# Weight chunks of the feed-forward, merge and output products: five matmuls (3 x 320, 512, 256 columns) in place of six of 288, with VectorE adding the two parts of the last 256 tokens

## The reference, cut to what matters

```python
def swiglu(x, w_in, w_out):
    gate, up = jnp.split(x @ w_in, 2, axis=-1)
    return (jax.nn.silu(gate) * up) @ w_out

def hybrid_layer(x, p, attn_fn, ...):
    x = x + 0.5 * swiglu(rms_norm(x, p['ffn1_norm']), p['ffn1_w_in'], p['ffn1_w_out'])
    h = rms_norm(x, p['mix_norm'])
    ... # attention (o_a), gated recurrence (o_b), short convolution (o_c)
    gates = jax.nn.sigmoid(g.reshape(n, t, N_BRANCH, D_MODEL))
    merged = (gates[:, :, 0] * (o_a @ wb[:WIDTH_A])
              + gates[:, :, 1] * (o_b @ wb[WIDTH_A:WIDTH_A + WIDTH_B])
              + gates[:, :, 2] * (o_c @ wb[WIDTH_A + WIDTH_B:]))
    x = x + merged @ p['w_out']
    x = x + 0.5 * swiglu(rms_norm(x, p['ffn2_norm']), p['ffn2_w_in'], p['ffn2_w_out'])
```

## Time and profile before

| what | value |
|---|---|
| median of 3 runs | 3013.25 us (3011.82 to 3015.27) |
| the profiled execution | 3012.57 us |
| its span, first to last instruction | 3010.9 us |
| TensorE, matmuls | 2959.2 us busy (98%), 21632 records |
| VectorE | 1465.2 us (49%) |
| ScalarE | 985.3 us (33%) |
| GpSimd | 119.0 us (4%) |
| HBM | 82 GB/s over the span |
| granted TensorE clock, mean | 0.991 of full |

### The profile page before, as it was taken

The page is one execution under the profiler, slowest core; times in us unless marked ns, Lnnn a source line. Parts: engine busy times, 40 slices in busy tenths (PEclk is TensorE's granted clock), DMA queues, the critical chain, the costliest instruction groups (busy, mean ns, idle before and its releaser), DMA issues.

```text
span 3010.9 us, 54957 instructions
## 1 busy us (share of the span) xinstructions
PE 2959.2 (98%) x21632; PEld 2862.5 (95%) x21632; DVE 1465.2 (49%) x2025; ACT 985.3 (33%) x1287; POOL 119.0 (4%) x104
## 2 busy tenths in 40 slices
PE   7999998999999999999999999989999999999999
PEld 6999998888899999999999999988888999999998
DVE  4434355555744544343444444566665454444434
ACT  4212133444633342121332111334445333321113
POOL 1000011000000010000100000100000000000001
PEclk9999999999999999999999999999999999999999
DMA  3222222333222222222222222223332222222222
GB/s 116 84 85 79 77 82 81 84 82 82 71 82 79 91 84 83 75 80 84 85 84 73 88 86 78 84 69 83 81 82 80 84 84 91 73 86 80 84 84 87
DMA packets 299022, 248.82 MB, mean 83 GB/s; under 512 B 20643, under 2 KB 296307, under 8 KB 298919
## 3 DMA queue, kind: packets, MB, share of 16 engines
q1 hardware_dynamic: 296775, 242.44, 26.0%
q0 software_dynamic: 2144, 4.98, 0.5%
HBM read 240.04 MB, written 7.34 MB: 82 GB/s over the span
## 4 chain that ended last, share of the span: by engine, by line
PE 94%; DVE 2%; ACT 1%; issue 1%; DVEq 0%; DMA 0%; POOLq 0%; ACTq 0%; SPq 0%
PE ps L448 85%; PE ps L671 2%; PE ps L616 2%; PE ps L700 1%; DVE tmp L1019 1%; PE ps L661 1%; PE ps L647 1%; PE ps L594 1%; PE ps L617 1%; PE ps L603 0%; PE ps L552 0%; PE ps L553 0%; PE ps L554 0%; DMA xin<-in_x_sample 0%; ACT whi L759 0%
## 5 line engine op out<-in xcount | busy, mean ns | idle before, releaser
L759 ACT ACTIVATE whi<-wraw 128x1024 fp32r<-128x1024 f32 (+1 forms) x456 | 475.1, 1044 | 1610.1 <-PE ps L448 1560.9
L448 PE MATMUL ps<-hh,whi 128*128 128x288 f32 x4480 | 967.1, 298 | 18.5 <-ACT vtok L857 6.1
L448 PE MATMUL ps<-hh,wlo 128*128 128x288 f32 x4480 | 961.9, 296 | 0.0
L448 PE MATMUL ps<-hl,whi 128*128 128x288 f32 x4480 | 961.5, 296 | 0.0
L1013 DVE TENSOR_TENSOR wlo<-wraw,whi 128x1024 fp32r<-128x1024 f32 (+1 forms) x456 | 548.4, 1205 | 457.4 <-ACT whi L759 456.3
L448 PEld LDWEIGHTS ps<-hh,whi 128*128 128x128 f32 x4480 | 724.9, 190 | 25.1 <-ACT vtok L857 6.3
L448 PEld LDWEIGHTS ps<-hh,wlo 128*128 128x128 f32 x4480 | 724.5, 189 | 0.0
L448 PEld LDWEIGHTS ps<-hl,whi 128*128 128x128 f32 x4480 | 724.3, 189 | 0.0
L1047 DVE TENSOR_TENSOR tmp<-tmp,ps 128x576 f32<-128x576 f32 x176 | 132.7, 754 | 509.3 <-PE ps L448 508.4
L448 PE MATMUL ps<-al,whi 128*128 128x288 f32 x1408 | 302.2, 296 | 0.0
L448 PE MATMUL ps<-ah,whi 128*128 128x288 f32 x1408 | 302.1, 296 | 0.0
(11 more groups left out here) (282 smaller groups left out, 2519.8 us busy)
## 6 DMA issues: line engine op xcount, KB each, us to landing
wraw<-in_ffn_w_in SPq DMA_DIRECT2D x88, 1024.0 KB
wraw<-in_ffn_w_out SPq DMA_DIRECT2D x32, 1024.0 KB
wraw<-in_w_in SPq DMA_DIRECT2D x28, 1024.0 KB
wraw<-in_w_in SPq DMA_DIRECT2D x56, 512.0 KB
wraw<-in_ffn_w_out SPq DMA_DIRECT2D x16, 768.0 KB
wraw<-in_w_branch SPq DMA_DIRECT2D x24, 512.0 KB
wraw<-in_w_out SPq DMA_DIRECT2D x9, 1024.0 KB
kv<-in_cache_k SPq DMA_DIRECT2D x128, 64.0 KB, 1.9
```

Source lines behind the costliest of these rows:

```text
L448: last = pe.matmul(ps[slot][:, half, 0:HF], weights, rhs[:, k, half * HF:(half + 1) * HF], start=(start and c == 0 and n == 0), stop=(stop ...
L759: act.activation(split_tile(whi, j, rowwise), raw_tile(slot, j, rowwise), ACT.Copy).then_inc(hi_ready, 1)
```

## The change

A chunk's 1728 columns are dealt out anew. The first 320 tokens (`NA`) go through three matmuls into the second part of bank 0 (columns 192 to 511). The last 256 (`NB`) go through one matmul of 512 columns, the high weight over the high part and the remainder side by side, which lands in bank 1 as two sums of 256, and one of 256 columns, the low weight over the high part, which is added to the first of the two. For that the high part and the remainder lie in one buffer (`hb`, `ab`, `ob`, `mb`). VectorE then has to add the second sum of 256: `scaled` multiplies 576 contiguous columns (192 to 767 of the slot) by the norm or the gate, multiplies the 256 of the second sum, and adds the two, with a drain before each step; `update` has a second multiply-add of 256 columns. The slot is freed by the last of these. The values and pairs stages go on with halves of 288.

```diff
@@ -37,6 +37,8 @@
+NA = 320
+NB = N - NA
...
-        hh = sb("hh", [P, KD, N], F32R)
-        hl = sb("hl", [P, KD, N], F32R)
+        hb = sb("hb", [P, 2, KD, N], F32R)
+        hh, hl = hb[:, 0, :, :], hb[:, 1, :, :]
...
+        def flat(k):
+
+            return ps[k][:, :, :].rearrange("p b n -> p (b n)")[:, 512 - NA:512 + NB]
+
...
-            def project(slot, w, chunks, rhs_hi, rhs_lo, start=True, stop=True, before=None):
-
+            def project(slot, w, chunks, buf, hi=0, before=None):
+
+                wide, both, rest = ps[slot][:, 0, 512 - NA:512], ps[slot][:, 1, 0:2 * NB], ps[slot][:, 1, 0:NB]
                 for c, k in enumerate(chunks):
                     if before is not None:
                         before(c)
                     wh, wl = whi[:, w % 2, c * P:(c + 1) * P], wlo[:, w % 2, c * P:(c + 1) * P]
-                    for n, (weights, rhs) in enumerate(((wh, rhs_hi), (wh, rhs_lo), (wl, rhs_hi))):
+                    first, end = c == 0, c == len(chunks) - 1
+                    pe.matmul(wide, wh, buf[:, hi, k, 0:NA], start=first, stop=False)
+                    pe.matmul(wide, wh, buf[:, 1 - hi, k, 0:NA], start=False, stop=False)
+                    pe.matmul(wide, wl, buf[:, hi, k, 0:NA], start=False, stop=end)
+                    pe.matmul(both.rearrange("p (a n) -> p a n", a=2), wh, buf[:, :, k, NA:N], start=first, stop=end, skip_group_check=True)
+                    last = pe.matmul(rest, wl, buf[:, hi, k, NA:N], start=False, stop=end, skip_group_check=True)
+                return last
...
+            def scaled(out, slot, by, spare):
+
+                dve.tensor_tensor(out, by, flat(slot), ALU.mult)
+                dve.drain()
+                dve.tensor_tensor(spare[:, 0:NB], by[:, NA:N], ps[slot][:, 1, NB:2 * NB], ALU.mult)
+                dve.drain()
+                return dve.tensor_tensor(out[:, NA:N], out[:, NA:N], spare[:, 0:NB], ALU.add)
...
-                        dve.scalar_tensor_tensor(out=two(xm), in0=cols(st.slot(k)), scalar=half, in1=two(xm), op0=ALU.mult, op1=ALU.add)\
+                        dve.scalar_tensor_tensor(out=xm, in0=flat(st.slot(k)), scalar=half, in1=xm, op0=ALU.mult, op1=ALU.add)
+                        dve.drain()
+                        dve.scalar_tensor_tensor(out=xm[:, NA:N], in0=ps[st.slot(k)][:, 1, NB:2 * NB], scalar=half, in1=xm[:, NA:N],
+                                                 op0=ALU.mult, op1=ALU.add)\
                             .then_inc(freed[st.slot(k)], 1)
...
-                            dve.tensor_tensor(two(pf[:, 0:N]), two(tmp[6][:, 0:N]), cols(st_in.slot(k)), ALU.mult)\
-                                .then_inc(freed[st_in.slot(k)], 1)
+                            scaled(pf[:, 0:N], st_in.slot(k), tmp[6][:, 0:N], tmp[2]).then_inc(freed[st_in.slot(k)], 1)
...
-                                dve.tensor_tensor(two(tmp[j][:, 0:N]), cols(mg.slot(k)), two(tmp[6][:, 0:N]), ALU.mult)\
+                                scaled(tmp[j][:, 0:N], mg.slot(k), tmp[6][:, 0:N], tmp[3])\
                                     .then_inc(freed[mg.slot(k)], 1)
...
-                                t = two(tmp[2 + j][:, 0:N])
-                                dve.tensor_tensor(t, two(tmp[j - 2][:, 0:N]), cols(mg.slot(k)), ALU.mult).then_inc(freed[mg.slot(k)], 1)
+                                t = tmp[2 + j][:, 0:N]
+                                scaled(t, mg.slot(k), tmp[j - 2][:, 0:N], tmp[3]).then_inc(freed[mg.slot(k)], 1)
```

More of the change, by code:

```diff
@@ L184, in build @@
         with ExitStack() as m:
[L185 to L186 removed]
+            ab = sb("ab", [P, 2, 8, N], F32R, m)
+            ah, al = ab[:, 0, :, :], ab[:, 1, :, :]
         with ExitStack() as m:
@@ L445, in project, with halves @@
                     wh, wl = whi[:, w % 2, c * P:(c + 1) * P], wlo[:, w % 2, c * P:(c + 1) * P]
-                    for n, (weights, rhs) in enumerate(((wh, rhs_hi), (wh, rhs_lo), (wl, rhs_hi))):
+                    first, end = c == 0, c == len(chunks) - 1
[5 more added lines that the diff above has]
+                return last
+            def halves(slot, w, chunks, start=True, stop=True):
+                for c, k in enumerate(chunks):
+                    wh, wl = whi[:, w % 2, c * P:(c + 1) * P], wlo[:, w % 2, c * P:(c + 1) * P]
+                    for n, (weights, rhs) in enumerate(((wh, hh), (wh, hl), (wl, hh))):
                         for half in range(2):
@@ L450, in project, with plain, plain_halves @@
                 return last
-            def plain(st, k, w, chunks, rhs_hi, rhs_lo, L, i=0, before=None):
+            def plain(st, k, w, chunks, buf, hi, L, i=0, before=None):
                 wait_weights(st, w, L, i)
                 wait_psum(st, k, L, i)
-                project(st.slot(k), w, chunks, rhs_hi, rhs_lo, before=before).then_inc(filled[st.slot(k)], 1)
+                project(st.slot(k), w, chunks, buf, hi, before=before).then_inc(filled[st.slot(k)], 1)
+            def plain_halves(st, k, w, L, i=0):
+                wait_weights(st, w, L, i)
+                wait_psum(st, k, L, i)
+                halves(st.slot(k), w, range(KD)).then_inc(filled[st.slot(k)], 1)
             def norm(st, n, L):
@@ L493, in ffn @@
                         for k in range(4):
-                            plain(st_out, k, k, range(kc), ah, al, L, i, before=hidden_ready if k == 0 else None)
+                            plain(st_out, k, k, range(kc), ab, 0, L, i, before=hidden_ready if k == 0 else None)
             pe.wait_ge(x_loaded, X_LOADS * 16)
@@ L595, in _ @@
                         last.then_inc(filled[pr.slot(k)], 1)
-                    plain(pr, 5, 3, range(KD), hh, hl, L, p)
-                    plain(pr, 6, 4, range(KD), hh, hl, L, p)
+                    plain_halves(pr, 5, 3, L, p)
+                    plain_halves(pr, 6, 4, L, p)
                     pe.wait_ge(kv_loaded, it * 512 + 256)
@@ L639, in _ @@
                     last.then_inc(filled[pr.slot(13)], 1)
-                    plain(pr, 14, 5, range(KD), hh, hl, L, p)
+                    plain_halves(pr, 14, 5, L, p)
                     pe.wait_ge(xc_ready, it + 1)
@@ L684, in _ @@
                     wait_psum(pr, 20, L, p)
-                    project(pr.slot(20), 6, range(4), hh, hl, stop=False)
+                    halves(pr.slot(20), 6, range(4), stop=False)
                     wait_weights(pr, 7, L, p)
-                    project(pr.slot(20), 7, range(4, KD), hh, hl, start=False).then_inc(filled[pr.slot(20)], 1)
+                    halves(pr.slot(20), 7, range(4, KD), start=False).then_inc(filled[pr.slot(20)], 1)
                     pe.wait_ge(vp_ready, it + 1)
@@ L716, in _ @@
                         for j in range(2):
-                            plain(mg, 4 * b + j, 4 * b + j, range(KD), hh, hl, L, i)
+                            plain(mg, 4 * b + j, 4 * b + j, range(KD), hb, 0, L, i)
                         pe.wait_ge(o_ready, L * 12 + 4 * (b + 1))
                         for j in range(2, 4):
-                            plain(mg, 4 * b + j, 4 * b + j, range(4 * b, 4 * b + 4), oh, ol, L, i)
+                            plain(mg, 4 * b + j, 4 * b + j, range(4 * b, 4 * b + 4), ob, 1, L, i)
                 with pe.Fori(0, 2) as i:
                     for k in range(4):
-                        plain(S["out"], k, k, range(KD), mh, ml, L, i, before=(lambda c: pe.wait_ge(m_ready, L * 8 + (c + 1))) if k == 0 else None)
+                        plain(S["out"], k, k, range(KD), mb, 1, L, i, before=(lambda c: pe.wait_ge(m_ready, L * 8 + (c + 1))) if k == 0 else None)
                 ffn("ffn2", 2, L)
@@ L1387, in _ @@
                             dve.wait_ge(gate_ready, L * 24 + i * 6 + (2 * b + j - 1))
-                            mt = merged[:, bass.ds(i * 2 + (j - 2), 1), :].rearrange("p a (b n) -> p (a b) n", b=2)
+                            mt = chunk(merged, i * 2 + (j - 2))
                             if b == 0:
-                                dve.tensor_tensor(mt, two(tmp[j - 2][:, 0:N]), cols(mg.slot(k)), ALU.mult).then_inc(freed[mg.slot(k)], 1)
+                                scaled(mt, mg.slot(k), tmp[j - 2][:, 0:N], tmp[3]).then_inc(freed[mg.slot(k)], 1)
                                 dve.drain()
                             else:
-                                t = two(tmp[2 + j][:, 0:N])
-                                dve.tensor_tensor(t, two(tmp[j - 2][:, 0:N]), cols(mg.slot(k)), ALU.mult).then_inc(freed[mg.slot(k)], 1)
+                                t = tmp[2 + j][:, 0:N]
+                                scaled(t, mg.slot(k), tmp[j - 2][:, 0:N], tmp[3]).then_inc(freed[mg.slot(k)], 1)
                                 dve.drain()
```

23 lines of the change are left out of this document (12 added, 11 removed).

## The result

The changed kernel takes 3030.65 us, the median of 4 runs (3027.34 to 3033.26); the kernel before takes 3012.98 us beside it, the median of 4. The ratio is 1.0057, with a 95% interval from 1.0042 to 1.0072: 17.7 us slower, where 3013.4 was forecast, and outside the range of 3003 to 3028. The profiled execution took 3030.31 us (span 3028.6), against 3012.57 (span 3010.9).

What follows compares the result with a forecast made beforehand. TensorE, busy for 98% of the span, was taken as the bound: matmul count times pace. Gain of 33.6 us kept and 33.7 us added give +0.1 us on the profiled 3012.57, median forecast 3013.4 us, range 3003 to 3028.

Steps and rivals of the forecast that it cites:

- One instruction's 13.3 ns is saved: Feed-forward, merge and output matmuls: a chunk falls from 800 to 786.7 ns, 2816 chunks worth 37.5 us.
- The term of what is added: VectorE's added operations make TensorE wait in feed-forwards, merge, output and layer turn: 33.7 us in all.
- e: VectorE's extra time for a `scaled`, two more operations of 256 columns with their gaps: 0.98 us.
- The merge groups: Merge: VectorE's addition delays the next group's weight split, 18.5 us over 22 groups, plus 1.3 in each layer's first group.
- The wait for the last of the merged values: Merge to output: three `scaled` lengthen TensorE's wait for `ml` from 1.0 to near 3 us, 5.9 us added.
- The in-tiles of steady state: Feed-forward in-tiles: VectorE's added work is covered with 0.5 us left, so TensorE doesn't wait.
- The turn of the layers: Turn of the layers and end: second multiply-add half covered by ScalarE's copy, 2 x 0.25 = 0.5 us, an estimate.
- the term for the starts of the feed-forwards: Four feed-forward starts, where TensorE already waits for the third tile's split: 4 x 0.98 = 3.9 us added.
- The gain lost beside waits: In 294 of 2816 chunks, just ahead of TensorE's waits, shorter matmuls give nothing; 33.6 of 37.5 us are kept.
- Rival 1: Slower: VectorE's two small operations cost more than their columns, e = 1.34, 13.7 us added, 3027; chance 0.15.
- Rival 2: Slower: only 2.5 ns go with a matmul instruction, not 13.3; 27.3 us lost, 3041; chance 0.08.
- Rivals 3 and 4: Faster: chains grow less, e = 0.76, 3005, chance 0.17; long streams hide the 13.3 ns, about 2904, chance 0.05.

Runs made afterwards that it cites:

- Experiment 1: Changed kernel with only the first VectorE operation kept in `scaled` and `update`, so the second sums are left out: 2989.95 us, ratio 0.9919 to the kernel before.
- experiment 5: Five one-run variants of the changed kernel's matmuls: 512 split into two 256s 3013.84 us, 512 read in one piece 3029.73, three other orders 3038.33, 3031.72, 3031.89.
- Experiment 2: Kernel before, six matmuls kept, with VectorE's added 256-column operations behind each multiply, results unused: 3050.09 us, ratio 1.0118.
- experiment 4: Changed kernel with ScalarE's weight copy moved ahead of the second gate's sigmoid in the merge: 3007.62 us; control, the same exchange in the kernel before: 3012.54 us.

## Why the prediction was wrong

- **The step that failed is "One instruction's 13.3 ns is saved"**, the term of -37.5 us (33.6 kept). Experiment 1 measures it at 23.2 us, so 14.3 us of it weren't there (4.5 either way). The working took the overhead of 288 and 256 columns and carried it to 512, which no row showed; 320 with 256 bears the rule out (experiment 5), the chunk with 512 doesn't. The traces account for nearly all of it: 2816 x 3.3 ns = 9.4 us since a chunk saves 10 ns and not 13.3, 2.6 for the part at 6.24 us before, where the change makes the tiles longer, and some 1.4 for out-tiles that save only 7 ns (6.34 to 6.35 us against 6.40). The bound was named, 2.5 ns (3041), but as a rival of its own at 0.08, with nothing between it and 13.3; the measured 8.2 lies there, and the range stopped at 3028.
- **The rule of the skill, against the trace.** The Trainium skill, "TensorE: Matmul & The Clock Gate", section "Back-to-back issue gap", gives 2.5 ns beside the columns, but for a matmul by itself, and says that in a stream of weight loads and matmuls both together set the spacing. The prediction left that out. By the 2.5 ns the matmuls alone would have saved 2816 x 2.5 ns = 7 us, an estimate from the Trainium skill's figure. Experiment 1 has 23.2: the measurement decides against it for this stream.
- **The term of what is added, 33.7 us, was nearly right.** Experiment 2 has 36.9. e was 0.99 for 0.98. The merge groups: 24 waits of 9.3 + 9.2 = 18.5 us as recorded, for 18.5 + 1.3. The wait for the last of the merged values: 3.0 to 3.1 us, for "near 3". VectorE's busy time: 1731.5 for 1741. The in-tiles of steady state wait for nothing, as said. The turn of the layers was put too low. TensorE's wait for the third tile's split there is 4.0 us in place of 1.9. Of these 2.1 us, 0.99 is the `scaled` that the term for the starts of the feed-forwards has; the other 1.1 stand against 0.25. From the last update's first operation to VectorE's first multiply of the new layer it is 16.07 us in place of 15.23, and 0.60 of these 0.84 are the second multiply-add with the gap ahead of it (0.17 + 0.43), of which the prediction took half to be covered. Where the rest comes from wasn't traced.
- **The gain lost beside waits, 3.9 us, isn't contradicted.** -23.2 + 36.9 = 13.7, and the two together cost 17.7, so 4.0 us of the gain don't arrive when both are there. But each of the three is known to 4.5 us only, so the agreement to 0.1 us is luck; 294 chunks at the measured 8.2 ns would be 2.4.
- So the miss of 17.6 us against the forecast is 14.3 of pace, 3.2 of added waits and 0.1 of the rest. (The three are counted on the difference to before, +17.7 for a forecast of +0.1, and none is known better than the 4.5 us above.) Two things that the sum had no term for may lie in the 3.2: the turn of the layers, and the lower clock behind the longer wait for the output's input, which experiment 2 shows at the same place, at 0.78 and 0.79 over 8 us; there the first output tile takes 7.17 us in layer 1 and 7.74 in layer 2, in place of 6.40, 2.1 us in all. These runs don't separate them.
- **The rivals.** Rival 1 (3027) came nearest by its number and was wrong in its cause: e wasn't 1.34. Rival 2 was right in its direction: 13.3 - 8.2 = 5.1 of its 10.8 ns were missing. Rivals 3 and 4 are out.

## What to carry to other kernels

A sum that comes out at nothing is the difference of two large terms, 34 us each here: a third off one of them is the whole result, so the range must carry each term's own bounds. A price that two sizes agree on is not yet the price of a third, larger one; and a pace is read in every loop of the trace, not in one, since a loop elsewhere can run at another. Where a shorter stream makes another engine's chain the bound, look at that engine's order first: one exchange on ScalarE brought 23 us back, and 56 tiles left as they were, 48 of them branch tiles, another 13 against the kernel before in the same series.

## What was not expected of the hardware

- The pace of one sequence of matmuls differs between loops of one program and is constant within each: 780 ns a chunk in one part and 800 in the others of the kernel before, and 786 or 793 for the out-tiles of the changed one. TensorE waits for nothing in those stretches. Nor does it go with TensorE's instructions alone: in the control of experiment 4, where only ScalarE's order in the merge differs from the kernel before, and in experiment 2, the part that ran at 780 ns runs at 800. Each kernel has one trace, so whether two executions of one kernel would agree isn't shown. The cause is open.
- Five fp32r matmuls of 320, 320, 320, 512 and 256 columns take 790 ns, 14 ns each over their 1728 columns at 2.4 GHz, whether the 512 is read in one piece or two, and whether the weights are grouped or not; only interleaving the 512 and the 256 with the 320s moved it, to 793.
- After a wait of some 3 us the clock fell to its lower level for part of the next 4 us (0.61 of full in the window) at one place, the output of layer 2; the same wait in layer 1 left it at 1.00 (window 1056 to 1060). Over all traces with that wait it fell in 11 of 14 places.
